# Two blocks on one core: 512-column matmuls in the ways down, and the second block's w_out on halves that are normed afterwards

## The reference, cut to what matters

```
def swiglu(x, w_gate_up, w_down):
    gate, up = jnp.split(x @ w_gate_up, 2, axis=-1)
    return (jax.nn.silu(gate) * up) @ w_down
```

```
mixed = jnp.concatenate([rmsnorm(attn, g_attn_out[l]),
                         rmsnorm(conv, g_conv_out[l])], axis=-1)
x = x + gt1 * (mixed @ w_out[l])
h = rmsnorm(x, g_ffn[l]) * (1.0 + sc2) + sh2
```

## Time and profile before

| | us |
|---|---|
| median of 3 runs | 1820.75 (1820.26 to 1820.97) |
| the profiled execution, its own time | 1821.4 |
| its span, first to last instruction | 1819.6 |
| TensorE busy | 1744.4 (96%) |
| VectorE busy | 1228.8 (68%) |
| ScalarE busy | 888.1 (49%) |
| GpSimd busy | 355.4 (20%) |

### The profile page before, as it was taken

How to read it: one execution, slowest core, us unless ns; L and a number is a source line. 1 busy time by engine, 2 the same in 40 slices (tenths; PEclk the granted TensorE clock), 3 DMA queues, 4 the chain that set the end, 5 groups by cost and what they waited for, 6 DMA issues and landing times.

```text
span 1819.6 us, 37064 instructions
## 1 busy us (share of the span) xinstructions
PE 1744.4 (96%) x16066; PEld 1661.9 (91%) x16066; DVE 1228.8 (68%) x2050; ACT 888.1 (49%) x1560; POOL 355.4 (20%) x308
## 2 busy tenths in 40 slices
PE   6999999999899999999999999989999998789997
PEld 6999988887899999999998888789999987789997
DVE  5886675766567775678576675665787575569964
ACT  5664435323346554565444432345565555356652
POOL 3552000000112651256100000011355200011110
PEclk9999999999799999999999999989999999889999
DMA  8655522211147565565552311014565542235442
GB/s 297 237 217 192 210 93 93 94 36 37 48 163 269 214 222 195 201 262 207 191 204 77 109 71 48 25 62 172 209 255 203 212 165 97 90 124 184 179 153 103
DMA packets 44498, 282.96 MB, mean 156 GB/s; under 512 B 6064, under 2 KB 6704, under 8 KB 17712
## 3 DMA queue, kind: packets, MB, share of 16 engines
q1 hardware_dynamic: 44336, 280.60, 42.3%
HBM read 279.53 MB, written 1.05 MB: 154 GB/s over the span
## 4 chain that ended last, share of the span: by engine, by line
PE 83%; DVE 11%; ACT 4%; issue 1%; DMA 1%; POOL 0%; SPq 0%; DVEq 0%; ACTq 0%; POOLq 0%
PE bank L489 20%; PE bank L491 20%; PE bank L490 20%; PE bank L975 7%; PE bank L1571 3%; DVE WL L480 2%; ACT WH L475 2%; PE bank L520 1%; PE bank L1838 1%; PE bank L1115 1%; DMA ring<-wst 1%; DVE XC L1044 1%; PE bank L1848 1%; PE bank L677 0%; DVE ML L1342 0%
## 5 line engine op out<-in xcount | busy, mean ns | idle before, releaser
L489 PE MATMUL bank<-XNH,WH 128*128 128x256 f32 (+1 forms) x2176 | 621.6, 286 | 20.6 <-DVE XNL L566 12.7
L480 DVE TENSOR_TENSOR WL<-ring,WH 128x2048 fp32r<-128x2048 f32 (+1 forms) x235 | 509.9, 2171 | 188.3 <-ACT WH L475 188.0
L491 PE MATMUL bank<-XNH,WL 128*128 128x256 f32 (+1 forms) x2176 | 617.7, 284 | 0.0
L490 PE MATMUL bank<-XNL,WH 128*128 128x256 f32 (+1 forms) x2176 | 615.7, 283 | 0.0
L475 ACT ACTIVATE WH<-ring 128x2048 fp32r<-128x2048 f32 (+1 forms) x235 | 406.3, 1730 | 232.9 <-PE bank L491 182.3
L489 PEld LDWEIGHTS bank<-XNH,WH 128*128 128x128 f32 x2176 | 414.2, 190 | 26.0 <-DVE XNL L566 12.7
L490 PEld LDWEIGHTS bank<-XNL,WH 128*128 128x128 f32 x2176 | 415.5, 191 | 0.0
L491 PEld LDWEIGHTS bank<-XNH,WL 128*128 128x128 f32 x2176 | 415.5, 191 | 0.0
L489 PE MATMUL bank<-HH,WH 128*128 128x256 f32 x880 | 246.4, 280 | 0.7 <-POOL HL L872 0.6
L490 PE MATMUL bank<-HL,WH 128*128 128x256 f32 x880 | 246.2, 280 | 0.0
L491 PE MATMUL bank<-HH,WL 128*128 128x256 f32 x880 | 246.1, 280 | 0.0
(11 more groups left out here) (466 smaller groups left out, 2513.4 us busy)
## 6 DMA issues: line engine op xcount, KB each, us to landing
ring<-wst SPq DMA_DIRECT2D x206, 1024.0 KB, 4.8
ring<-wst SPq DMA_DIRECT2D x80, 704.0 KB, 4.2
LP<-lp SPq DMA_DIRECT2D x1, 1872.0 KB, 8.5
LP<-lp SPq DMA_DIRECT2D x1, 1792.0 KB, 8.8
X<-xin SPq DMA_DIRECT2D x2, 512.0 KB, 4.5
out<-X SPq DMA_DIRECT2D x4, 256.0 KB, 2.6
C<-cst SPq DMA_DIRECT2D x1, 193.0 KB, 10.6
AL<-cst SPq DMA_DIRECT2D x1, 192.0 KB, 10.7
```

The lines of the kernel that those rows point to most:

```text
L480: e.do.tensor_tensor(WL[:, slot[q], 0:n], ring[:, i % NSLOT, 0:n], WH[:, slot[q], 0:n].bitcast(F32), ALU.subtract).then_inc(*w_dve.up("low ...
L489: e.do.matmul(o, WH[:, s, cols], xh, start=first, stop=False)
L490: e.do.matmul(o, WH[:, s, cols], xl, start=False, stop=False)
L491: return e.do.matmul(o, WL[:, s, cols], xh, start=False, stop=last)
```

## The change

In the five ways down the hidden activations' high and low parts lie side by side in one array (HP). For output tiles 0 to 6 a new function `wide` issues two matmuls instead of three: the high weights once over both parts, 512 columns into the whole bank, and the low weights over the high part into the bank's first half. DVE then adds both halves of the bank to the residual, one after the other, the second waiting for the first. Output tile 7 stays with `three`.

In the second block's tail w_out takes the halves before they are normed: ACT multiplies by the gain while it takes the high part, and the low parts are made of that. Each half of w_out goes to its own half of bank m (m = 0 to 7, banks 6 and 7 for the last two). The spread root is copied out of PSUM by ACT ("root"), and DVE multiplies each half of each output tile by it and adds it with gt1 to the residual: four instructions for each m where there was one. The sums of norm 0 move behind the next tile of the input projection on TensorE, those of norm 1 behind all six attention halves. The low part of the last w_out block moves from behind m = 1's addition to behind the additions of the attention half for m = 0 to 5 and of the convolution half for m = 0 and 1; that of the feed-forward's first block moves behind all additions.

```diff
         if s == "norm1" and k == 0:
-            return done["conv"] == steps["conv"] and done["first"] >= 4
+            return done["conv"] == steps["conv"] and done["first"] >= 6
...
-                HH = part_c.enter_context(nc.sbuf_tensor("HH", [128, NF, T], F32R))
-                HL = part_c.enter_context(nc.sbuf_tensor("HL", [128, NF, T], F32R))
+                HP = part_c.enter_context(nc.sbuf_tensor("HP", [128, NF, 2, T], F32R))
...
+        HH, HL = HP[:, :, 0, :], HP[:, :, 1, :]
...
+        def wide(e, b, q, cols, x, first, last):
+            s = slot[q]
+            e.do.matmul(b[:, :], WH[:, s, cols], x.rearrange("p s t -> p (s t)"), start=first, stop=False)
+            return e.do.matmul(b[:, 0:T], WL[:, s, cols], x[:, 0, :], start=False, stop=last)
...
-                        m = three(e, b[:, 0:T], q, slice(k * 128, k * 128 + 128), HH[:, kk, :], HL[:, kk, :], kk == 0, kk == NF - 1)
+                        at = slice(k * 128, k * 128 + 128)
+                        if n < KT - 1:
+                            m = wide(e, b, q, at, HP[:, kk, :, :], kk == 0, kk == NF - 1)
+                        else:
+                            m = three(e, b[:, 0:T], q, at, HH[:, kk, :], HL[:, kk, :], kk == 0, kk == NF - 1)
...
-                        if f == 4:
-                            e.do.scalar_tensor_tensor(X2[:, n, :], bank[n][:, 0:T], gt2[:, n:n + 1], X2[:, n, :], ALU.mult,
-                                                   ALU.add).then_inc(*f_dve.up("add", f, n))
-                        else:
-                            e.do.scalar_tensor_tensor(X[:, n, :], bank[n][:, 0:T], 0.5, X[:, n, :], ALU.mult,
-                                                   ALU.add).then_inc(*f_dve.up("add", f, n))
+                        xt, by = (X2[:, n, :], gt2[:, n:n + 1]) if f == 4 else (X[:, n, :], 0.5)
+                        if n < KT - 1:
+                            e.do.scalar_tensor_tensor(xt, bank[n][:, T:2 * T], by, xt, ALU.mult, ALU.add).then_inc(*f_dve.up())
+                            e.wait_ge(*f_dve.last())
+                        e.do.scalar_tensor_tensor(xt, bank[n][:, 0:T], by, xt, ALU.mult, ALU.add).then_inc(*f_dve.up("add", f, n))
...
+        roots = RV2[:, 0:512]
+        scaled = RV2[:, 512:1024].rearrange("p (n t) -> p n t", t=T)
         def norm_squares(i):
             return MS2[:, 1024 * i:1024 * i + 1024]
@@ -2337,6 +2351,8 @@
         def pe_norm2(e, i):
             b, sq = bank[6 + i], norm_squares(i)
+            if i == 0:
+                yield
             e.wait_ge(*n_act[i].on("sq"))
             e.wait_ge(*b_dve.on("x2", KT - 1))
             e.wait_ge(*q_act.on("values", 3))
@@ -2346,94 +2362,140 @@
                     m = e.do.matmul(b[:, c:c + 1], sq[:, s:s + 128], ones[:, 0:1], start=n == 0, stop=n == 3)
             m.then_inc(*n_pe[i].up("sums"))
             yield
-            yield
+            if i:
+                yield
             e.wait_ge(*n_dve[i].on("rstd"))
             pe_rows(e, n_pe[i], ("rows",), b, SM[:, 142 + 6 * i:144 + 6 * i])
             yield
-        def act_norm2(e, i):
+        def act_norm2(e, i, gn):
+            if i:
+                act_y2(e, i, gn)
             for n in range(4):
                 e.wait_ge(*(c_dve.on("y", n) if i else a_act[n].on("y", 1)))
                 if i == 0:
                     e.wait_ge(*q_pe.on("values", 3))
                 e.do.activation(norm_squares(i)[:, T * n:T * n + T], Y2[:, 4 * i + n, :], ACT.Square).then_inc(*n_act[i].up("sq"))
-            yield
-            yield
+            if i:
+                act_y2_scaled(e, i, gn)
+            yield
+            if i == 0:
+                act_y2(e, i, gn)
+                act_y2_scaled(e, i, gn)
+            yield
+            e.wait_ge(*n_pe[i].on("rows"))
+            e.do.activation(roots[:, T * i:T * i + T], bank[6 + i][:, 0:T], ACT.Copy).then_inc(*n_act[i].up("root"))
+            yield
+        def act_y2(e, i, gn):
             for n in range(4):
                 yh, yl = y2_parts(4 * i + n)
-                e.wait_ge(*n_dve[i].on("y", n))
-                e.do.activation(yh, Y2[:, 4 * i + n, :], ACT.Copy).then_inc(*n_act[i].up("yh", n))
-            yield
-        def y2_low(e, signal, i, n):
-            yh, yl = y2_parts(4 * i + n)
-            e.wait_ge(*n_act[i].on("yh", n))
-            e.do.tensor_tensor(yl, Y2[:, 4 * i + n, :], yh.bitcast(F32), ALU.subtract).then_inc(*signal.up("yl", n))
+                e.wait_ge(*(c_dve.on("y", n) if i else a_act[n].on("y", 1)))
+                e.do.activation(yh, Y2[:, 4 * i + n, :], ACT.Copy, scale=spc(gn, n)).then_inc(*n_act[i].up("yh", n))
+        def act_y2_scaled(e, i, gn):
+            e.wait_ge(*n_act[i].last())
+            for n in (0, 2):
+                e.do.activation(Y2[:, 4 * i + n, :], Y2[:, 4 * i + n, :], ACT.Copy, scale=spc(gn, n)).then_inc(*n_act[i].up("scaled", n))
         def dve_norm2(e, i, gn):
+            if i:
+                dve_y2(e, i, gn)
             yield
             e.wait_ge(*n_pe[i].on("sums"))
             dve_rsqrt(e, n_dve[i], bank[6 + i][:, 0:2], 2, 1.0 / 512, EPS, 140 + 6 * i, ("rstd",))
             yield
+            if i == 0:
+                dve_y2(e, i, gn)
+            yield
+        def dve_y2(e, i, gn):
+            for n in (1, 3):
+                yh, yl = y2_parts(4 * i + n)
+                e.wait_ge(*n_act[i].on("yh", n))
+                e.do.scalar_tensor_tensor(yl, Y2[:, 4 * i + n, :], spc(gn, n), yh.bitcast(F32), ALU.mult, ALU.subtract).then_inc(*n_dve[i].up("yl", n))
+        def pool_norm2(e, i):
+            for n in (0, 2):
+                yh, yl = y2_parts(4 * i + n)
+                e.wait_ge(*n_act[i].on("scaled", n))
+                e.do.tensor_tensor(yl, Y2[:, 4 * i + n, :], yh.bitcast(F32), ALU.subtract).then_inc(*n_pool[i].up("yl", n))
+            yield
+            yield
+            yield
+        def pe_out2_half(e, m, i):
+            q = turn_of("w_out_2", 0, ("two", m // 2))
             for n in range(4):
                 k = 4 * i + n
-                e.wait_ge(*n_pe[i].on("rows"))
-                e.do.scalar_tensor_tensor(Y2[:, k, :], Y2[:, k, :], spc(gn, n), bank[6 + i][:, 0:T], ALU.mult, ALU.mult).then_inc(*n_dve[i].up("y", n))
-                if n % 2:
-                    y2_low(e, n_dve[i], i, n)
-            yield
-        def pool_norm2(e, i):
-            yield
-            yield
-            for n in (0, 2):
-                y2_low(e, n_pool[i], i, n)
-            yield
-        def pe_out2_part(e, m, k0, k1):
-            q = turn_of("w_out_2", 0, ("two", m // 2))
-            for k in range(k0, k1):
                 yh, yl = y2_parts(k)
-                e.wait_ge(*(n_dve if k % 2 else n_pool)[k // 4].on("yl", k % 4))
+                e.wait_ge(*(n_dve if n % 2 else n_pool)[i].on("yl", n))
                 at = k * 256 + m % 2 * 128
-                t = three(e, bank[m % 6][:, 0:T], q, slice(at, at + 128), yh, yl, k == 0, k == KT - 1)
-            if k1 == KT:
-                t.then_inc(*b_pe.up("out", m))
+                t = three(e, bank[m][:, T * i:T * i + T], q, slice(at, at + 128), yh, yl, n == 0, n == 3)
+            t.then_inc(*b_pe.up("out" if i else "out0", m))
         def pe_out2_first(e):
             for m in range(6):
                 if m % 2 == 0:
                     e.wait_ge(*low_on(turn_of("w_out_2", 0, ("two", m // 2))))
                 e.wait_ge(*(q_act.on("tile", 22 + m) if m < 2 else a_act[m - 2].on("y", 1)))
-                pe_out2_part(e, m, 0, 4)
+                pe_out2_half(e, m, 0)
+                yield
+            for m in range(2):
+                e.wait_ge(*b_dve.on("taken", m))
+                pe_out2_half(e, m, 1)
                 yield
         def pe_out2(e):
-            for m in range(KT):
-                if m == 6:
+            for m in range(2, KT):
+                if m < 6:
+                    e.wait_ge(*b_dve.on("taken", m))
+                else:
                     e.wait_ge(*low_on(turn_of("w_out_2", 0, ("two", 3))))
-                if m >= 6:
-                    e.wait_ge(*b_dve.on("add", m - 6))
-                pe_out2_part(e, m, 4 if m < 6 else 0, KT)
+                    e.wait_ge(*n_act[m - 6].on("root"))
+                    pe_out2_half(e, m, 0)
+                pe_out2_half(e, m, 1)
+        def dve_out2_half(e, m, i):
+            q = scaled[:, i, :]
+            e.wait_ge(*n_act[i].on("root"))
+            e.wait_ge(*b_pe.on("out" if i or m >= 6 else "out0", m))
+            e.wait_ge(*b_dve.last())
+            e.do.tensor_tensor(q, bank[m][:, T * i:T * i + T], roots[:, T * i:T * i + T], ALU.mult).then_inc(
+                *(b_dve.up() if i else b_dve.up("taken", m)))
+            e.wait_ge(*b_dve.last())
+            e.do.scalar_tensor_tensor(X2[:, m, :], q, gt1[:, m:m + 1], X2[:, m, :], ALU.mult, ALU.add).then_inc(
+                *(b_dve.up("add", m) if i else b_dve.up()))
+        def dve_out2_first(e):
+            for m in range(8):
```

(23 more changed lines are left out.)

5 lines of the change are left out of this document (3 added, 2 removed).

## The result

The changed kernel takes 1806.49 us (median of four, 1802.95 to 1808.37) beside 1820.71 before, a ratio of 0.9918 with a 95% interval of 0.9905 to 0.993: 14.2 us faster where 28.9 were forecast. That is half a microsecond above the upper end of the stated range, 1806. The repeat in the experiments gave 1806.06 beside 1820.62, again 0.9918 (0.9905 to 0.9932). The profiled execution is the longest of the four, 1808.37 with a span of 1806.5.

What follows compares the result with a forecast made beforehand. TensorE, busy 96% of the span, was taken as the bound. 1821.4 less 13.8 (ways) and 15.2 (tail) gave 1792.4 profiled, median 0.65 lower: 1791.8 us; range from 1784 less 1 us to 1806, forecast's own 1787 to 1796.

Steps and rivals of the forecast that it cites:

- Where time counts: Whole kernel: with TensorE busy 96% of the span, savings count where it streams without a gap or waits, almost nowhere else.
- the 35 extra additions: Ways down: DVE's added additions, 0.43 to 0.48 us each, are hidden; uncovered they would cost 17 us.
- The ways: Five ways down: each pair of matmuls 18.5 ns less than three, 14.2 us in all, 13.8 after a wait for POOL.
- the 512-column matmul: Ways down: the joined fp32r matmul of the high weights costs 216.2 ns, the 256-column one keeps 117.3.
- the reading of L975: Ways down: unsplit 32-bit matmuls at 216.2 ns, as long as 512 columns stream, taken as showing a toll of only 3 ns.
- the toll: Ways down: 10.6 ns of each 117.3, read as the part of a weight load that a 107 ns stream does not cover.
- Rivals 1: Ways down: the toll is the instruction's, 10.6 ns per matmul whatever its length; ways give 8.0, kernel 1797.6 us; chance 0.20.
- Rival 3: Ways down: a 512-column matmul runs as two of 256 with their tolls; ways give nothing, kernel 1805.6 us; chance 0.06.
- The end of each way is as it was: Ways down: no change at a way's end, because output tile 7 keeps one addition.
- The tail: Second block's tail: the last root starts 16.4 us earlier, less 1.2 for a half clock, so 15.2 us gained.
- the bounds: Second block's tail: gain between 11 (two half-clock stretches of 3.3 us each) and 17 (additions of 0.90).
- a DVE half: Second block's tail: each addition of a half is two dependent DVE instructions of 0.48 us, 0.96 together.

Runs made afterwards that it cites:

- The repeat: The changed kernel itself measured and profiled once more, nothing altered: 1806.06 us beside 1820.62 before, ratio 0.9918.
- the second probe: Changed kernel plus unused matmuls behind the last way down, varying what is read and written: 512 columns fp32r 234 ns, 16-bit 216, unsplit 32-bit 216 a record.
- the summing kernel: Changed kernel with the squares for the last root summed by TensorE instead of POOL: 1806.26 us, ratio to before 0.991.
- the kernel with both edits: Changed kernel with the last root's squares summed by TensorE instead of POOL and unused matmuls filling TensorE's waits behind them: 1806.99 us, ratio to before 0.9923.

## Why the forecast was right in direction and twice too large

**Where time counts.** Right: TensorE's stream and its waits; the 35 extra additions cost nothing in the ways themselves.

**The ways: 4.0 instead of 13.8.** The term that was mis-sized is the 512-column matmul, 229 ns instead of 216.2. The step that failed is the reading of L975: 512 clocks long, it was taken for a stream of 512 columns, and its 3 ns for what is left of the toll. By the second probe it is 256 columns at half the pace. The 10.6 ns of a 256-column matmul are no toll of the load or the instruction but some 10% on each 32-bit column, so there was next to nothing to save by joining matmuls. Rivals 1 and 3 stand on either side of the result: 229 is neither 224 nor 234, and 4.0 neither 8.0 nor 0. Rival 3's 234 is what the matmul takes alone, though nothing is split. That the time lies within a microsecond of rival 3's 1805.6 is chance: the ways gave 4.0 where that rival has none, and the tail about as much less than its 15.2.

**The end of a way.** "The end of each way is as it was" was wrong by 0.4 us: tile 6's second addition stands ahead of two low parts, and the last addition starts 0.96 us behind the way's last matmul instead of 0.60. TensorE waits 0.43 for it at the second block.

**The tail: 12.1 less 0.7 instead of 15.2.** In the old clock's time (1.14 later than the profile after), forecast and found: tile 22 at 1557.1 and 1557.8; the second sums at 1573.9 and 1574.7; the last projection matmul's end at 1590.7 and 1592.9; the last addition's end at 1592.8 and 1596.9; the last root's start at 1595.1 and 1599.4. Up to the sums the order came out as worked. Then two terms failed. Behind the sums a half clock from 1576.0 to 1579.4 cost 1.5 in the halves (the repeat and the summing kernel have none there, and reach the second spread 1.5 sooner behind the sums): it was among the bounds, with 1.2 allowed. And a DVE half was priced at 0.96, twice the instruction of the earlier trace rows, which reads a bank, while the second instruction of a half reads SBUF alone. Four of the last eight halves lie beside POOL and take 1.46 to 1.55 from start to start, and the last addition ends 3.9 behind TensorE instead of 2.1.

**Not foreseen.** The half clock at the second block's beginning; the stretch from the fourth way to tile 18's end is 1.8 us longer than before in the profile, and up to 3 in others. The changed kernel's four executions differ by 5 us beside 0.7 before, but in the later comparisons the kernel before differs by 5 to 7 us itself (9 to 15 executions), so that spread tells nothing of the change.

## What to carry to other kernels

Before a matmul is widened, ask what the time above a column per clock hangs on: the fp32r stream here paid it by the column, and joining instructions saves next to nothing of that; 16-bit columns did not pay it. A price may be borrowed from another instruction only if it reads the same number of columns, and, on DVE, from the same memories: moving an operand from a bank to SBUF put it in POOL's way. Moving 16 small sums off the head of a queue, a matter of a few lines, was worth 6.9 us in one profile, more than the five rewritten ways with their 4.0.

## What the runs showed of the hardware

An fp32r stream runs at some 0.457 ns a column at the full clock (117 ns for 256, 234 for 512) but at one column per clock at half clock (214.6 for 258); 16-bit data of 512 columns take 216. A DVE instruction of 0.48 us with both inputs in SBUF takes 0.98 beside a POOL addition; one with an input in a bank keeps its 0.42. In the kernel with both edits the clock fell to its lower level (0.50 from 1591.9 us) after TensorE had run one-column sums for 3 us, and the 27 full matmuls behind took 5.4 us instead of 3.2.
